# Moving attention's division out of the attention stage of an eight-core decoder layer

## The reference, cut to what matters

```python
def layer(x):
    xn = rmsnorm(x)
    qa, ka, va, qr, kr, vr, gr, ga, gb = split(xn @ w_in)
    # branch A: 16 heads of 64; three dilated patterns share one softmax
    for (window, r) in ((128, 1), (512, 4), (2048, 16)):
        o, m, den = banded_causal_softmax(q, k, v, window, r)
    y_att = (sum(w * o) / sum(w)) @ w_att       # w = den * exp(m - m_all)
    # branch B: retention, 4 heads, chunks of 128, swish gate
    y_ret = (rmsnorm(retention(qr, kr, vr)) * silu(gr)) @ w_ret
    x = x + (sigmoid(ga) * y_att + sigmoid(gb) * y_ret) @ w_out
    return x + moe(rmsnorm(x))                  # 32 experts, top 2 of one group
```

## Time and profile before

| | |
|---|---|
| median of 3 runs | 1603.95 us (1598.38 to 1607.03) |
| the profiled execution's own time | 1600.68 us |
| its span (slowest core, core 6) | 1596.2 us |
| spans of the eight cores | 1581.8 to 1596.2 us |
| PE busy | 1371.4 us (86%) |
| DVE / ACT / POOL busy | 765.3 / 695.0 / 763.7 us |
| DMA queue of POOL (q0), packets | 29280, 48.6% of 16 engines |
| DMA queue of SP (q1), packets | 76066, 28.2% of 16 engines |

### The profile page before, as it was taken

The page is one execution under the profiler, slowest core; times in us unless marked ns, Lnnn a source line. Parts: engine busy times, 40 slices in busy tenths (PEclk is TensorE's granted clock), DMA queues, the critical chain, the costliest instruction groups (busy, mean ns, idle before and its releaser), DMA issues.

```text
span 1596.2 us, 29866 instructions; the slowest of 8 cores (1581.8 to 1596.2 us)
## 1 busy us (share of the span) xinstructions
PE 1371.4 (86%) x10037; PEld 787.3 (49%) x10037; DVE 765.3 (48%) x1239; ACT 695.0 (44%) x1191; POOL 763.7 (48%) x874
## 2 busy tenths in 40 slices
PE   4889998888879999999999899999999746476575
PEld 2344447777654444444444344444445435355463
DVE  3687774767556656555656411111355662121122
ACT  3576667887753444434443411111233543223232
POOL 1379991332236657666756312221226645354353
PEclk9999998999999999999999899999999867788797
DMA  9747865777865678999984299785964785999985
GB/s 213 212 92 131 166 145 152 175 175 171 176 146 100 112 107 127 127 131 146 125 134 123 55 293 175 119 131 111 261 211 166 212 303 151 265 254 256 261 188 92
DMA packets 105502, 267.03 MB, mean 167 GB/s; under 512 B 43354, under 2 KB 65370, under 8 KB 98818
## 3 DMA queue, kind: packets, MB, share of 16 engines
q0 software_dynamic: 29280, 124.30, 48.6%
q1 hardware_dynamic: 76066, 140.76, 28.2%
HBM read 285.71 MB, written 116.65 MB: 252 GB/s over the span
## 4 chain that ended last, share of the span: by engine, by line
PE 69%; DMA 14%; DVE 4%; issue 4%; ACT 4%; POOL 3%; SPq 1%; POOLq 0%; DVEq 0%; ACTq 0%
PE ps L169 69%; DMA arena<-xn,idx 8%; DMA zret<-arena 5%; ACT arena L169 4%; DVE arena L169 3%; POOL arena L169 3%; DMA arena<-x 1%; DMA cfs_sb<-cfs 1%; SPq L169 1%; DVE arena L167 1%; DMA vp<-arena 0%; ACT L169 0%; DVEq L156 0%; DVE logit L169 0%; POOL wb L169 0%
## 5 line engine op out<-in xcount | busy, mean ns | idle before, releaser
L169 PE MATMUL ps<-arena 128*128 128x512 bf16 (+5 forms) x8208 | 1275.5, 313 | 75.1 <-ACT arena L169 30.2
L169 PEld LDWEIGHTS ps<-arena 128*128 128x128 bf16 (+1 forms) x8208 | 677.4, 102 | 583.4 <-issue 121.5
L169 ACT ACTIVATE arena<-ps 128x512 bf16<-128x512 f32 (+5 forms) x600 | 422.5, 719 | 445.8 <-PE ps L169 416.7
L169 POOL TENSOR_TENSOR arena<-arena 128x512 bf16<-128x512 f32 (+4 forms) x274 | 347.8, 1278 | 296.5 <-DVE arena L169 243.0
L169 DVE TENSOR_TENSOR arena<-ps,arena 128x512 f32<-128x512 f32 (+4 forms) x420 | 235.2, 572 | 337.9 <-PE ps L169 153.5
L169 PE MATMUL ps<-cbs_sb,arena 128*128 128x128 bf16 x1408 | 130.8, 232 | 111.6 <-DMA arena<-xn,idx 76.3
L169 DVE SCALAR_TENSOR_TENSOR arena<-arena,ps 128x512 f32<-128x512 f32 x176 | 115.6, 683 | 192.8 <-PE ps L169 191.3
L169 PEld LDWEIGHTS ps<-cbs_sb,arena 128*128 128x128 bf16 x1408 | 100.3, 104 | 180.8 <-issue 152.0
L169 ACT ACTIVATE arena<-arena 128x8 f32<-128x8 f32 (+5 forms) x225 | 148.6, 665 | 60.1 <-DVE arena L169 24.5
L169 DVE TENSOR_TENSOR arena<-arena 128x1024 bf16<-128x1024 bf16 (+9 forms) x176 | 131.7, 756 | 70.6 <-ACT arena L169 63.6
L169 POOL DMA_INDIRECT out<-arena,idx x48 | 76.3, 1591 | 122.8 <-ACT arena L169 68.8
(11 more groups left out here) (60 smaller groups left out, 340.6 us busy)
## 6 DMA issues: line engine op xcount, KB each, us to landing
wb<-wexp POOLq DMA_DIRECT2D x60, 768.0 KB, 16.0
arena<-wb SPq DMA_DIRECT2D x30, 1536.0 KB, 16.0
arena<-x SPq DMA_DIRECT2D x32, 512.0 KB, 7.2
arena<-vx POOLq DMA_DIRECT2D x12, 768.0 KB, 15.1
arena<-wri POOLq DMA_DIRECT2D x8, 1024.0 KB, 23.2
zret<-arena SPq DMA_DIRECT2D x16, 512.0 KB, 19.0
arena<-zret SPq DMA_DIRECT2D x4, 2048.0 KB, 17.2
out<-arena SPq DMA_DIRECT2D x16, 512.0 KB, 8.2
```

What stands on the lines that cost most here:

```text
L169: ins = getattr(engobj, meth)(*a, **kw)
```

## The change

Attention no longer divides. For each head `head_out` writes the numerator (64 x 2048, float32, 512 KB) to `num_d` and one row of denominators (8 KB) to `den_d`; `den_shift`, `den_act` and `z_out` go. At the start of retention all denominators are read as one 128 x 256 tile, inverted by one DVE `reciprocal` at step 1 and written to `rden_d`. The product is made where the merge reads it: `div_load` fetches a 128 x 512 piece of numerators (256 KB, one transfer) and its inverse denominators, each row of `rden_d` spread over 64 partitions (two transfers of 128 KB written); `div_mul` (DVE) multiplies them into `za[c][:, pr, :]`. There are 32 such pieces: 8 each for chunks 0 and 1 in steps 45 to 56 of retention, from four buffers that are first filled at step 42, and 8 each for chunks 2 and 3 between the first nine units of the merge, from three buffers.

Beside this: of the four batches masked on PE two stay there (`n_ in (3, 5)`) and two go to DVE; the conversion per pair in attention goes, and retention converts up to step 55 instead of 47 (six more); merge tiles move in SBUF (`mT[3]`, `wo`, `sga[1]`, `sgb[1]`, `hTt`, `lTt`), `za[3]` gets a place of its own, and `load_za` goes.

```diff
+        def head_out(pr, e):
+            h, r0, d0, i = 2 * pr + e, e * 64, 64 - e * 64, (2 * pr + e) % NXO
+            p.dma(num_d[h * 64:(h + 1) * 64, :], xo[i][r0:r0 + 64, :], reads=Rxo[i], writes=[Rnum[h]], semkey=("zatt", i))
+            p.dma(den_d[h:h + 1, :], xo[i][d0:d0 + 1, :], reads=Rxo[i], writes=[Rdend[h]], semkey=("xin", i))
...
-                todo.setdefault(g + 1, []).append(lambda: (osb_copy(pr, eh, 3), den_shift(pr, eh, 1)))
-                if eh == 1:
-                    for hf in range(2):
-                        for lag, f in ((1, lambda hf=hf: den_act(pr, hf, AF.Ln, 1.0)), (3, lambda hf=hf: den_act(pr, hf, AF.Exp, -1.0)),
-                                       (5, lambda hf=hf: z_out(pr, hf) if pr < 7 else deferred.append(lambda: z_out(pr, hf)))):
-                            todo.setdefault(g + lag + 4 * hf, []).append(f)
+                todo.setdefault(g + 1, []).append(lambda: (osb_copy(pr, eh, 3), head_out(pr, eh)))
...
-                    if n_ == 9:
-                        convert(1)
...
-            queue.append((pr, eh, n_, S_item(pr, eh, kind, j, n_ in (2, 3, 4, 5))))
+            queue.append((pr, eh, n_, S_item(pr, eh, kind, j, n_ in (3, 5))))
...
+        def den_rec():
+            OP("dve", "reciprocal", out=dall, in_=dall, reads=[Rdall], writes=[Rdall])
+            p.dma(rden_d.rearrange("h (a b) -> (h a) b", a=8), dall, reads=[Rdall], writes=[Rrden], semkey="gqkb")
...
+        def div_load(c):
+            pr, i = dv[0] % 8, dv[0] % len(nb)
+            dv[0] += 1
+            cs = slice(c * 512, c * 512 + 512)
+            p.dma(nb[i], num_d[pr * 128:(pr + 1) * 128, cs], reads=Rnum[2 * pr:2 * pr + 2], writes=[Rnb[i]], semkey=("vp", i))
+            for e in range(2):
+                p.dma(rb[i][e * 64:(e + 1) * 64, :], rden_d[2 * pr + e, cs].partition_broadcast(64), reads=[Rrden], writes=[Rrb[i][e]],
+                      semkey=(("zero", i // 2, i % 2), ("qz", i // 2, i % 2, False))[e])
+
+        def div_mul(c):
+            pr, i = dv[1] % 8, dv[1] % len(nb)
+            dv[1] += 1
+            OP("dve", "tensor_tensor", out=za[c][:, pr, :], in0=nb[i], in1=rb[i], op=ALU.mult, reads=[Rnb[i]] + Rrb[i],
+               writes=[Rza[c][pr]])
...
-                if deferred:
-                    deferred.pop(0)()
+                if s_ == 1:
+                    den_rec()
+                if s_ == 42:
...
+                    for u_ in range(4):
+                        div_load(0)
+                if 45 <= s_ < 57:
+                    for _ in range(1 + (s_ % 3 == 0)):
+                        div_mul(dv[1] // 8)
+                        if dv[0] < 16:
+                            div_load(dv[0] // 8)
                 pending = pending[take:]
-                if s_ % 4 != 1 and s_ < 48:
+                if s_ % 4 != 1 and s_ < 56:
                     convert(1)
...
+                pi = 5 * un + n
+                if pi >= 4 and dv[1] < 16 and (pi % 2 == 0 if dv[1] < 8 else pi % 3 == 0):
+                    div_mul(2 + dv[1] // 8)
+                    if dv[0] < 16:
+                        div_load(2 + dv[0] // 8)
```

More of the change, by code:

```diff
@@ L319, in build_nc @@
     wb_d = nc.dram_tensor("wb", [NE, 128, 6144], BF16, kind="Internal").ap()
-    zatt_d = nc.dram_tensor("zatt", [D, S], BF16, kind=skind).ap()
+    num_d = nc.dram_tensor("num", [D, S], F32, kind="Internal").ap()
+    den_d = nc.dram_tensor("den", [16, S], F32, kind="Internal").ap()
+    rden_d = nc.dram_tensor("rden", [16, S], F32, kind="Internal").ap()
     zret_d = nc.dram_tensor("zret", [2 * D, S], BF16, kind=skind).ap()
@@ L763, in build_nc @@
         xo = [alloc([128, S], F32, Rxo[i]) for i in range(NXO)]
[L764 to L767, removed]
+        Rnum = [p.res(f"num{h}") for h in range(16)]
+        Rdend = [p.res(f"dend{h}") for h in range(16)]
         slot = [0]
@@ L973, in build_nc @@
             g += 1
-        deferred = []
         for g in sorted(todo):
@@ L1019, in build_nc, with div_bufs @@
         assert apos[0] <= 167 * KB, apos[0]
+        areset(92 * KB, 96 * KB)
+        Rdall = p.res("dall")
+        dall = alloc([128, 256], F32, [Rdall])
+        Rrden = p.res("rden")
+        p.dma(dall, den_d.rearrange("h (a b) -> (h a) b", a=8), reads=Rdend, writes=[Rdall], semkey="rawtab")
+        Rnb = [p.res(f"nb{i}") for i in range(4)]
+        Rrb = [[p.res(f"rb{i}_{e}") for e in range(2)] for i in range(4)]
+        nb, rb, dv = [], [], [0, 0]
+        def den_rec():
+            OP("dve", "reciprocal", out=dall, in_=dall, reads=[Rdall], writes=[Rdall])
+            p.dma(rden_d.rearrange("h (a b) -> (h a) b", a=8), dall, reads=[Rdall], writes=[Rrden], semkey="gqkb")
+        def div_bufs(at):
+            assert dv[0] == dv[1]
+            del nb[:], rb[:]
+            for i, k in enumerate(at):
+                areset(k * KB)
+                nb.append(alloc([128, 512], F32, [Rnb[i]]))
+                rb.append(alloc([128, 512], F32, Rrb[i]))
+            dv[:] = [0, 0]
+        def div_load(c):
[11 more added lines that the diff above has]
+               writes=[Rza[c][pr]])
         INNER = ps[:, 3, 0:128]
@@ L1141, in build_nc @@
         za, zr = {}, {}
-        Rza = [[p.res(f"za{c}")] for c in range(NG)]
+        Rza = [[p.res(f"za{c}_{k}") for k in range(8)] for c in range(NG)]
         Rzr = [[p.res(f"zr{c}")] for c in range(NG)]
@@ L1195, in build_nc @@
                 if s_ == 57:
-                    areset(168 * KB)
-                    z_alloc(0)
-                    load_za(0)
+                    zr_alloc(0, 176)
                     load_zr(0)
[L1200 to L1204, removed]
+        zr_alloc(1, 64)
+        load_zr(1)
+        div_bufs((56, 60, 124))
+        for u_ in range(3):
+            div_load(2)
+        za_alloc(2, 80)
+        zr_alloc(2, 88)
+        load_zr(2)
+        za_alloc(3, 152)
+        areset(104 * KB)
         wm.append(alloc([128, 40, 128], BF16, Rwm[2]))
@@ L1208, in build_nc @@
         RmT = [[p.res(f"mT{c}_{k}") for k in range(8)] for c in range(NG)]
-        mT = [alloc([128, 8, 512], BF16, RmT[c]) for c in range(NG)]
+        mT = [alloc([128, 8, 512], BF16, RmT[c]) for c in range(NG - 1)]
+        areset(160 * KB)
         Rwo = [p.res(f"wo{i}") for i in range(2)]
         wo = [alloc([128, 8, 512], BF16, [Rwo[0]])]
-        areset(192 * KB)
+        areset(116 * KB, 124 * KB)
         wo.append(alloc([128, 8, 512], BF16, [Rwo[1]]))
@@ L1282, in build_nc @@
                 areset(168 * KB)
-                z_alloc(LC)
-                load_za(LC)
+                mT.append(alloc([128, 8, 512], BF16, RmT[LC]))
+                zr_alloc(LC, 176)
                 load_zr(LC)
```

30 lines of the change are left out of this document (9 added, 21 removed).

## The result

The changed kernel takes **1687.15 us** (median of 4 runs, 1685.94 to 1693.1) against 1603.24 for the kernel before on the same chip: ratio 1.0533, 95% interval 1.0494 to 1.0571. The direction was as forecast, the size was not (1619, range 1573 to 1645). The profiled execution took 1688.21 us, its slowest core is core 7. Some executions, whatever the kernel, lose several per cent on one half of the cores at a lower clock; all times and ratios leave these out.

The account below looks back on a forecast made before the run. PE bounds retention and merge; in attention no engine is full, PE and ACT wait on each other. Terms -35 + 20 + 27 + 4 + 5 = +21, less 3 for catching up, gave +18 on 1600.7: 1619 us, range 1573 to 1645.

Parts of the forecast that it names:

- Attention, division out: Attention: seven pairs of heads that hold a division each get 3.32 us shorter, -23.2 us.
- Mask by DVE: Attention: 32 of 64 mask biases leave PE at 0.38 us each, -12.2 us where PE sets the pace.
- The bound: Attention's sum of -35 us had bounds -23 and -42, as some unexplained PE gaps may go with the conversions.
- Retention, products: Retention, step 46: DVE waits for the first loads, issued behind a slow store and beside conversions; PE loses 20 us.
- the first wait: Retention, step 46: DVE stands at its first products, free at 817 instead of 794.2; PE loses 20 us.
- The equal counts of q0 and q1: Sign in retention: the two DMA queues take turns one for one, so equal packet counts between DVE's two stops.
- Retention, conversions and merge weights: Retention, to step 53: load 11 lands only after q0's ten transfers; DVE waits 14 to 44 us, 27 us taken.
- the forecast's rate: Retention: once q0 is empty, q1's some 2000 remaining packets go at 150 to 200 per us, 10 to 13 us.
- Clock: Retention and merge: two stretches where PE idles bring a lower granted clock, +4 us, bounds 0 and 10.
- Merge: Merge: late loads of chunks 2 and 3 hold DVE, mostly covered by 17 us of PE's lead; +5 us, bounds 0 to 25.
- Rival D: Merge is stuck as well, chunk 3 costing 25 us instead of 5: 1639 us, chance 0.08.
- Rival C: Retention and merge: no starving, loads get many rows per turn or land ahead, DVE never waits: 1566 us, chance 0.08.

Follow-up runs that it names:

- e9_mask_conv: Kernel before, division kept, with two instead of four batches per head masked on PE and attention's six conversions moved to retention: 1612.09 us, ratio 1.0019.
- e17_norden: Changed kernel without the loads of inverse denominators (buffers set to a constant): steps 45 to 57 102.4 us, merge 206.7; whole time not comparable.
- e3_convearly: Changed kernel with twelve conversions in attention, two per pair, and retention converting only up to step 39: 1660.77 us, ratio 1.0338.
- e2_noload: Changed kernel without the 96 loads for the products, buffers set to one: steps 45 to 57 83.8 us, merge 198.8; whole time not comparable.
- e1_rows: Changed kernel, inverse-denominator loads reading 64 different numerator rows instead of one row: steps 45 to 57 138.1 us, merge 225.9; whole time not comparable.
- e15_rows4k: Changed kernel, each retention load bringing both chunks of a pair (4 KB rows, half the packets, same bytes): 1677.85 us, ratio 1.0442.
- e6_conv6: Changed kernel with the six conversions back in attention, one per pair, and retention converting up to step 47: 1678.82 us, ratio 1.0459.
- e8_late3: Changed kernel, in the merge chunk 2's first three loads ahead of zr[1], zr[2] later, chunk 3's products later: 1685.03 us, ratio 1.0519.
- e16_merge: Changed kernel with the load order of e8_late3 and the 64 DRAM copies of e4_copies: 1670.49 us, ratio 1.0395.
- e4_copies: Changed kernel, inverse denominators written to DRAM 64 times so every partition reads its own row: 1674.28 us, ratio 1.0418.

## Why the prediction was wrong

The forecast was a change of +18 us, the result is +84. Of the 66 us between them 36 lie in the merge (+41 instead of +5) and most of the rest in steps 45 to 57 of retention (+77 instead of 48, with the clock).

*Attention, division out; Mask by DVE* (-35): the sum was right (-34), its parts were not, so this hit is in part luck. The division is worth 15 alone and not 23, but 33 as the last of the three parts (216.4 in `e9_mask_conv` against 183.4). The mask is worth 4 to 9 and not 12 once the division is out, and the conversions, set at nothing, 9.5 to 14.5. The bound said that some of PE's gaps might go with them; it should have been a term.

*Retention, products* (20): the first wait came as described and cost 22.69 us of PE. The equal counts of q0 and q1, the 18.31 us that stay in `e17_norden` and `e3_convearly`, where it is gone, bear its mechanism out.

*Retention, conversions and merge weights* (27): this is the step that failed, in the price of the loads. It let the packets of q1 that are left when q0 has run empty end it at "150 to 200 per us". In place of one more wait came three large ones (9.41, 18.61 and 14.41 us), 42 in sum. The 4096 packets of 2 KB took some 65 us of the engines (72.8 of q1, less the 7.6 that it takes for four stores of `zret` in `e2_noload`), where the forecast's rate makes 20 to 27 of them. With distinct rows 39 of the 65 remain (28.4% of 164 in `e1_rows`, less 7.6), and without the loads of `rden` no later wait is left. The number of turns does not set these waits: `e15_rows4k` and `e17_norden` have about as many packets on q1 (4854 and 4388), and the one keeps 31 us of later waits, the other none. The reckoning by packet time: 92 us before, six conversions at 5 us each (79 us of q0 in `e6_conv6`, 109 after) and 65 make 187 against 182 measured, in a stretch of 109. By the forecast's own rate it would be 142 to 149, or 33 to 40 us too much, no more than the 47 that the two terms held. So it is the price that made the miss, more than the way of counting.

*Clock* (+4, bounds 0 to 10): PE idles more often and longer than twice; 92.62 us instead of 80.50 in retention and 204.11 instead of 199.00 in the merge (924 matmuls against 922) make +17.

*Merge* (+5, bounds 0 to 25): this failed as well, by the same price and by the place of the loads. PE waits for 36 us. Rival D named the mechanism, DVE stuck behind products that nobody needs yet (12.96 us, gone in `e8_late3` and `e16_merge`, where chunk 3's products come late), but priced it at 25 for chunk 3 alone and gave it 8 in 100. The larger wait is the one for chunk 2, 20.04 us at 1002 to 1022: I had put its load behind `zr[1]` only, but with three buffers all loads from the fourth on go out behind `zr[2]` too, and PE's lead of two units (17 us) was spent by then. Without the loads of `rden` the merge is 33 us shorter; order alone gave 15 (`e8_late3`), order and distinct rows 27 (`e16_merge`).

Sum of the medians: -34 in attention, +77 in steps 45 to 57, +41 in the merge, the rest -4: +80, against 83.9 between the slowest cores. Rival C is out: DVE waited for 182 us. The rule of the Trainium skill behind it ("DMA: Bandwidth & Descriptors", section "Queues, rings and completion order") was misread as well. It lets an engine drain a whole packet from either queue's ring before it changes, so q0's pieces would come several to a turn like q1's rows, and by it too the loads could be held up; equal counts alone do not tell its packets of several from turns of one. The times of the packets do: from 640 to 700 us before, a packet of q0 starts within 5 ns of the end of 1065 of the 1082 rows of `zret` on q1, so after one row the turn is over, and the skill's packet length does not agree with this trace.

## What to carry to other kernels

Before work is sent through DRAM, multiply the DMA share of the stretch that it goes through by its length, add the new packets' time, and compare with the length: where much lies above, most of it comes out as waits. Here a longer lead only moved them, and order and fewer packets gave back a part (15 of 41 us, 16 of 77). Where little lies above, a load can still be late behind what stands ahead of it in its own queue and beside it in the other one, as the first wait shows. Take packet time from a row of the same kind in the same company, since the loads here took two to three times what the rate of an undisturbed queue had let me expect. And where engines wait for each other in turn, one part of a change alone may give nothing, or twice as much as the last: price the parts together, or run them.

## What the runs showed of the hardware

One row of DRAM read by 64 partitions is slow: by difference (72.8 less 25.7 us of q1, core 7), the `rden` loads of steps 41 to 57 take 47 us for 2048 packets of 2 KB on 16 engines, about 370 ns each; with distinct rows throughout the 4096 packets took 39 us, about 150 ns each. Beside conversions two queues move equal numbers of packets whatever their size (677 and 678 in 33 us, at 3.68 and 0.68 MB). POOL's power costs 163 us over 64 x 1024, about 160 ns per element of a partition, while one over 128 x 1 takes 0.57 us. And 8192 pieces of 1 KB written by one transfer (`e4_copies`) cost retention 31 us.
